# Dilated attention: the mean squares of queries and keys as four 64x64 matmuls in one group with the transposes of V and P, and the copy of V behind Exp

## The reference, cut to what matters

```python
q = rms_norm_2(q.reshape(B, S, N_HEADS, HEAD_DIM), q_norm_g[l]).astype(jnp.float32) * HEAD_DIM ** -0.5
k = rms_norm_2(k.reshape(B, S, N_HEADS, HEAD_DIM), k_norm_g[l]).astype(jnp.float32)
v = v.reshape(B, S, N_HEADS, HEAD_DIM).astype(jnp.float32)
for window, dilation in DILATION_GROUPS:
    o_g, lse_g = dilated_window_attention(q, k, v, slopes, window, dilation)
...
mix = jax.nn.softmax(jnp.stack(lses), axis=0)
o = jnp.einsum('gbsh,gbshd->bshd', mix, jnp.stack(outs))
```

## Time and profile before

| | |
|---|---|
| median of 3 runs | 1976.29 us (1975.88 to 1976.3) |
| the profiled execution | 1976.66 us, of which its span is 1974.7 us |
| TensorE busy | 1967.1 us (100%), 9778 matmul passes |
| TensorE weight loads busy | 1620.0 us (82%) |
| VectorE busy | 1188.5 us (60%) |
| ScalarE busy | 843.3 us (43%) |
| DMA, mean over the span | 95 GB/s |
| table loads of lines 1424 and 1428 | 8 and 8, 1283 ns each |
| Ln of line 1424 | 16 of 128x512, 689 ns each |

### The profile page before, as it was taken

One profiled execution on the slowest core, in us unless ns is written; L12 is line 12 of the kernel. 1 busy time (PEld: TensorE's weight loads), 2 busy tenths in 40 slices (PEclk: granted clock), 3 DMA queues, 4 the chain that ended last, 5 costly groups with the idle time before them and its releaser, 6 DMA issues.

```text
span 1974.7 us, 25252 instructions
## 1 busy us (share of the span) xinstructions
PE 1967.1 (100%) x9778; PEld 1620.0 (82%) x9778; DVE 1188.5 (60%) x1800; ACT 843.3 (43%) x1368; POOL 12.6 (1%) x18
## 2 busy tenths in 40 slices
PE   9999999999999999999999999999999999999999
PEld 8787888888888779888888987777788898888887
DVE  4345754444466765444445686777897547774764
ACT  4534543333246744323323426777544334442431
POOL 0000000000000000000000000000000000000000
PEclk9999999999999999999999999999999999999999
DMA  5122232323223113232422332222232313332321
GB/s 187 61 100 86 75 107 75 118 96 117 75 100 146 55 54 110 94 104 68 148 86 86 107 99 84 86 86 86 86 96 97 128 45 115 98 96 75 117 96 64
DMA packets 51895, 188.04 MB, mean 95 GB/s; under 512 B 5761, under 2 KB 6017, under 8 KB 51138
## 3 DMA queue, kind: packets, MB, share of 16 engines
q1 hardware_dynamic: 51778, 186.43, 29.0%
HBM read 184.31 MB, written 2.10 MB: 94 GB/s over the span
## 4 chain that ended last, share of the span: by engine, by line
PE 97%; DVE 1%; ACT 1%; issue 0%; DMA 0%; SPq 0%; DVEq 0%; ACTq 0%
PE ps L398 19%; PE ps L400 19%; PE ps L399 19%; PE ps L427 10%; PE ps L429 10%; PE ps L428 10%; PE ps L451 1%; PE ps L866 1%; PE ps L899 1%; PE ps L880 1%; PE ps L844 1%; PE ps L785 1%; PE ps L771 1%; PE ps L756 1%; PE ps L631 0%
## 5 line engine op out<-in xcount | busy, mean ns | idle before, releaser
L398 PE MATMUL ps<-HH,WH 128*128 128x512 f32 (+1 forms) x1776 | 659.3, 371 | 0.4 <-DVE WL L1643 0.4
L400 PE MATMUL ps<-HH,WL 128*128 128x512 f32 (+1 forms) x1776 | 650.6, 366 | 0.0
L399 PE MATMUL ps<-HL,WH 128*128 128x512 f32 (+1 forms) x1776 | 650.5, 366 | 0.0
L1034 ACT ACTIVATE WH<-WR 128x1024 fp32r<-128x1024 f32 x305 | 321.1, 1058 | 651.4 <-PE ps L400 373.2
L1643 DVE TENSOR_TENSOR WL<-WR,WH 128x1024 fp32r<-128x1024 f32 x304 | 370.3, 1225 | 192.2 <-ACT WH L1034 185.5
L398 PEld LDWEIGHTS ps<-HH,WH 128*128 128x128 f32 x1776 | 334.9, 189 | 61.7 <-issue 7.9
L400 PEld LDWEIGHTS ps<-HH,WL 128*128 128x128 f32 x1776 | 334.9, 189 | 54.9
L399 PEld LDWEIGHTS ps<-HL,WH 128*128 128x128 f32 x1776 | 335.1, 189 | 54.6 <-issue 1.9
L427 PE MATMUL ps<-WH,HIDH 128*128 128x512 f32 x620 | 241.6, 390 | 0.0
L429 PE MATMUL ps<-WL,HIDH 128*128 128x512 f32 x620 | 241.2, 389 | 0.0
L428 PE MATMUL ps<-WH,HIDL 128*128 128x512 f32 x620 | 241.2, 389 | 0.0
(11 more groups left out here) (248 smaller groups left out, 2018.3 us busy)
## 6 DMA issues: line engine op xcount, KB each, us to landing
WR<-in_up SPq DMA_DIRECT2D x108, 512.0 KB, 3.6
WR<-in_down SPq DMA_DIRECT2D x86, 512.0 KB, 3.5
WR<-in_in SPq DMA_DIRECT2D x56, 512.0 KB, 3.6
WR<-in_swa_in SPq DMA_DIRECT2D x10, 512.0 KB, 4.6
WR<-in_gla_in SPq DMA_DIRECT2D x9, 512.0 KB, 4.8
WR<-in_gla_v SPq DMA_DIRECT2D x8, 512.0 KB, 3.5
WR<-in_gla_g SPq DMA_DIRECT2D x8, 512.0 KB, 4.6
WR<-in_gla_out SPq DMA_DIRECT2D x8, 512.0 KB, 3.7
```

The lines of the kernel that those rows point to most:

```text
L398: e.matmul(ps, wh, hi[:, c, cols], start=c == 0, stop=False)
L399: e.matmul(ps, wh, lo[:, c, cols], start=False, stop=False)
L400: y = e.matmul(ps, wl, hi[:, c, cols], start=False, stop=c == x.n - 1)
L1034: e.activation(x.wh[:, 0:n], m.WR[:, u % RAW, 0:n], AF.Copy).then_inc(*k.mark("whi", u))
```

## The change

On TensorE, `norm_qk` no longer multiplies with the whole of `blk`. The squares of each head (64 partitions) are multiplied with the head's 64x64 block alone, in four matmuls: `s` is the head, which gives the rows of the array and the bank (3 or 6), and `s ^ j` the columns and the half of the bank's partitions, so that the four use the four quadrants of the array. One semaphore step follows the last of them. The transposes of V come right behind them, and those of P behind these; the first two chunks of the product of Q, which stood between, now follow. V is transposed into bank 7 in place of bank 3.

On ScalarE, Ln is taken of each quadrant, four of 64x512 in place of two of 128x512, and the copy of the transposed V moves from between Ln and Exp to behind Exp.

```diff
@@ tensor: t_second
     def norm_qk(c):
-        for j, b in ((0, 3), (1, 6)):
+        for j in range(2):
             e.wait_ge(*k.on("qksq", c, j))
-            e.wait_ge(*k.on(*k.free[b]))
-            e.matmul(ps[b][:, :], cst(m, "blk"), m.AT2[:, j, :], start=True, stop=True).then_inc(*k.mark("blk", c, j))
-            k.free[b] = ("qkln", c, j)
+            for s, b in ((0, 3), (1, 6)):
+                rows, side = slice(64 * s, 64 * s + 64), slice(64 * (s ^ j), 64 * (s ^ j) + 64)
+                if j == 0:
+                    e.wait_ge(*k.on(*k.free[b]))
+                x = e.matmul(ps[b][side, :], cst(m, "blk")[rows, rows], m.AT2[rows, j, :], start=True, stop=True,
+                             skip_group_check=True)
+        x.then_inc(*k.mark("blk", c))
+        for s, b in ((0, 3), (1, 6)):
+            k.free[b] = ("qkln", c, 1, s)
 
     def turn_v(c):
         e.wait_ge(*k.on("ev", at["qkv"] + 3 * c + 2))
-        e.wait_ge(*k.on(*k.free[3]))
+        e.wait_ge(*k.on(*k.free[7]))
         for t in range(4):
-            x = e.transpose(ps[3][:, t * 128:(t + 1) * 128], m.TMP[:, 0, t * 128:(t + 1) * 128], ident)
+            x = e.transpose(ps[7][:, t * 128:(t + 1) * 128], m.TMP[:, 0, t * 128:(t + 1) * 128], ident)
         x.then_inc(*k.mark("v2t", c))
-        k.free[3] = ("v2", c)
+        k.free[7] = ("v2", c)
@@ tensor: the loop over c
-        product(e, k, u, hi, lo, 2, 0, ev="ae", c1=2)
         turn_v(c - 1)
         if c > 1:
             turns(c - 2)
-        product(e, k, u, hi, lo, 2, 0, ev="ae", c0=2)
+        product(e, k, u, hi, lo, 2, 0, ev="ae")
         score(c - 1)
@@ scalar: a_second
     def norm_qk(c):
-        for j, b in ((0, 3), (1, 6)):
-            e.wait_ge(*k.on("blk", c, j))
-            e.activation(m.AT2[:, j, :], ps[b][:, :], AF.Ln, bias=eps(m)).then_inc(*k.mark("qkln", c, j))
+        e.wait_ge(*k.on("blk", c))
+        for j in range(2):
+            for s, b in ((0, 3), (1, 6)):
+                rows, side = slice(64 * s, 64 * s + 64), slice(64 * (s ^ j), 64 * (s ^ j) + 64)
+                e.activation(m.AT2[rows, j, :], ps[b][side, :], AF.Ln, bias=eps(m)[rows, :]).then_inc(
+                    *k.mark("qkln", c, j, s))
+        for j in range(2):
+            e.wait_ge(*k.on("qkln", c, j, 1))
+            e.activation(m.AT2[:, j, :], m.AT2[:, j, :], AF.Exp, scale=-0.5).then_inc(*k.mark("qkex", c, j))
         turn_v(c)
-        for j in range(2):
-            e.wait_ge(*k.on("qkln", c, j))
-            e.activation(m.AT2[:, j, :], m.AT2[:, j, :], AF.Exp, scale=-0.5).then_inc(*k.mark("qkex", c, j))
```

More of the change, by code:

```diff
@@ L1397, in turn_v @@
             e.wait_ge(*k.on("pv", "a", 2 * c - 5))
-        e.activation(m.V2[:, c % 3, :, :], ps[3][:, :].rearrange("p (t f) -> p t f", t=4), AF.Copy).then_inc(
+        e.activation(m.V2[:, c % 3, :, :], ps[7][:, :].rearrange("p (t f) -> p t f", t=4), AF.Copy).then_inc(
             *k.mark("v2", c))
```

## The result

| | before | changed |
|---|---|---|
| median of 20 runs each, same chip | 1975.95 us (1973.86 to 1976.76) | 1979.28 us (1977.4 to 1979.95) |
| ratio | | 1.0017, 95% interval 1.0011 to 1.0023 |
| span of the profiled execution | 1974.7 us | 1975.6 us (its time 1977.4 us) |

The kernel became 3.3 us slower, 0.17%. That is less than the 0.2% which the prediction counts as no change, but 0.1 us above its range, which ended at 1979.2 us. The forecast was +0.4 us. I compare distances inside the attention.

What follows compares the result with a forecast made beforehand. TensorE's own time and its waits were taken to bound the kernel. 7 x 0.15 - 0.6 = +0.4 us on 1976.29 us gave 1976.7 us, range 1974.2 to 1979.2 us.

Steps and rivals of the forecast that it cites:

- item 4: ScalarE's four Ln, 0.60 us apart, hold bank 6: TensorE stands still 0.77 us, +0.15 us per chunk in chunks 1 to 7.
- Item 1: Mean squares on TensorE: four quadrants run at once, done at 1.11 us against 1.73, 0.62 us gained per chunk without waits.
- Rival B: Mean squares on TensorE: quadrants run two at a time, group 1.88 us, +7.3 us, 1983.6 us; chance 0.07.
- Items 2 and 3: TensorE's seam back to fp32r: nothing to gain; V's transposes directly behind: VectorE's copy in time except chunk 1, 0.2 us lost.
- rival C: Ln on 64 partitions is short, 405 ns at 0.31 us distance: -4.9 us, 1971.4 us; chance 0.08.
- The bound from above: Upper case for the distance between two Ln: 0.69 us, no overlap, +0.42 us per chunk, +2.3 us in all.
- the bound of 0.50 us: Lower case for the distance between two Ln: larger overlap, as for Exp without bias; -0.15 us per chunk, -1.7 us in all.
- Item 5: Chunk 0, no P and so no wait for bank 6; scores start at 7.16 us against 7.77: -0.6 us in all.
- Item 6: V's copy behind Exp on ScalarE: two extra Ln (1.2 us) hide in the wait it removes; scores stay covered; nothing.
- rival D: Scores of chunks 1 to 7 wait for K or a copy of P: some us slower; chance 0.03.

## Why the prediction was wrong in size

The mechanism was right: the quadrants' gain is taken back inside the group by the wait for bank 6. What failed is the size of a term of item 4, the distance from one Ln to the next, 0.71 us where 0.60 was put in.

- *Item 1, the quadrants.* Forecast 0.09 + 1.02 us, measured the same to 0.01 us. Rival B is out. By the rule of the Trainium skill, "TensorE: Matmul & The Clock Gate" (Part 3, on what overlaps), that a weight load overlaps running matmuls only on other rows of the array, the group would have taken twice 0.85 us. The eight weight loads stand within 0.21 us and the group took 1.02 us, so here the measurement goes against it.
- *Items 2 and 3, seam and V's copy.* V was turned 1.11 us behind the product in chunk 2 as forecast, and 0.2 us later in chunk 1; swallowed by the wait, as forecast. In the run with whole matmuls the order by itself cost nothing.
- *Item 4, the step that failed.* First Ln at t = 1.25 (forecast 1.23), duration 0.68 us (0.69): right, and rival C is out. The distance was taken from a pair whose source and destination start at partition 0 both times, 0.60 us. Measured 0.71 us. Three times per chunk that is 0.33 us. The other 0.05 us: TensorE resumed 0.11 us after the last Ln (1246.95 to 1247.06), not 0.06, which was read behind a VectorE instruction. Bank 6 came at 4.17 in place of 3.78, so TensorE stood still for 1.16 us in place of 0.77, and the product of Q began at 4.89 in place of 4.51: **0.38 us** more in each of seven chunks, **2.7 us**. The bound from above, 0.69 us, was meant as "no overlap"; the true distance lies 0.02 us outside even this.
- *Bounds.* Both bounds left chunk 0 at -0.6 us, though its scores wait for K and so for the fourth Ln: with 0.69 us the sum is about +2.6 us, not +2.3. And the bound of 0.50 us misread its row: the two Exp (0.63 us each, 1.15 us together) overlap by the same 0.10 us, they are only shorter.
- *Item 5, chunk 0.* Forecast -0.6, measured -0.26 us. It is the same term: K was ready 0.36 us later than forecast (t = 7.46), and the scores wait for K (t = 7.51, from 1195.88 to 1203.39; forecast 7.16).
- *Item 6, V's copy behind Exp.* ScalarE's copies of P began at t = 6.91 (6.6 forecast, 6.70 before), and in chunks 1 to 7 no scores waited for them or for K, so rival D is out. The copy of V has a price that the item left out: back in front of Exp it makes K of chunk 0 later and costs 0.6 us there, by the trace of that run.

With 0.71 and 0.11 us put in, item 4 gives 7 x 0.53 and item 5 about -0.3: +3.4 us, against 3.3 measured. That the wait for the last Ln makes the loss is shown from both ends: no wait with the six matmuls back or with two whole Ln, a shorter one with bank 6 first. How much of it is the longer distance is worked out from the rows; no run has four Ln on halves at 0.60 us, since each step between two of them changes a half.

## What to carry to other kernels

A faster matmul gains nothing if the engine then waits for its result to leave PSUM: work out first what the readers cost, and ask how soon the bank is wanted again. Here 1.36 us of other work between the two turned +3.3 us into -3.7 us. If a result has to change halves on the way, do it in the step that nobody waits for. And a distance between two instructions, which enters a sum several times, should be read from a pair whose first partitions change in the same way, or be bounded beyond "no overlap".

## What the runs showed of the hardware

Two ACTIVATE in a row overlap by about 0.10 us if the second reads from the same first partition as the first did and writes to the same one (three Ln of 510 columns in 1.84 us, 0.69 us each). The Trainium skill, "ScalarE: Activation LUTs", on what a table load costs, gives about 93 ns for back-to-back ones. The whole Ln agree with it within 0.02 us (0.69 us long, 0.58 us apart).

If the first partition changes on either side, between 0 and 64 in all these runs, the overlap is gone: 0.12 us more per change. This was so with a bias and without, out of PSUM and out of SBUF. Other first partitions weren't tried, nor was why a change costs this.

The number of partitions made no difference to an ACTIVATE's time: 0.68 us for 64 and 0.69 us for 128 at 512 columns. Between the end of the last Ln and TensorE's next weight load lay 0.11 us.
